# First norm's squares on ScalarE, opening loads in smaller pieces

## The reference

```python
def rmsnorm(x, g):
    x32 = x.astype(F32)
    y = x32 * lax.rsqrt(jnp.mean(x32 * x32, axis=-1, keepdims=True) + EPS)
    return (y * g.astype(F32)).astype(x.dtype)
...
qa, ka, va, qi, ki, wi, cqlat, ckv, kr = split_cols(u @ w_in, AB_SPLITS)   # u = rmsnorm(h, g_mix)
...
k_new = rope(rmsnorm(ka.reshape(nb, t, A_KV_HEADS, A_HEAD_DIM), g_ak), pos)
...
log_a = -RG_C * r * jax.nn.softplus(-lam.astype(F32))                        # layer 1
```

## Time and profile before

| | before |
|---|---|
| median of 3 runs | 2961.33 us (2958.95 to 2961.46) |
| profiled execution, span | 2955.7 us |
| TensorE busy | 2905.3 us, 98% |
| VectorE busy | 1441.9 us, 49% |
| ScalarE busy | 1057.9 us, 36% |
| GpSimd busy | 203.9 us, 7% |
| loads of the weight stream | 742 of 512 KB |
| mean granted clock of TensorE | 0.992 |

### The profile page before, as it was taken

How to read it: one execution, slowest core, us unless ns; L and a number is a source line. 1 busy time by engine, 2 the same in 40 slices (tenths; PEclk the granted TensorE clock), 3 DMA queues, 4 the chain that set the end, 5 groups by cost and what they waited for, 6 DMA issues and landing times.

```text
span 2955.7 us, 45474 instructions
## 1 busy us (share of the span) xinstructions
PE 2905.3 (98%) x18745; PEld 2840.7 (96%) x18745; DVE 1441.9 (49%) x1483; ACT 1057.9 (36%) x1190; POOL 203.9 (7%) x108
## 2 busy tenths in 40 slices
PE   6999899999999999999999999999999999999999
PEld 6999769999999999999999999899999999999999
DVE  7568553643344344334365774446443443443443
ACT  3243432433233233233234642424433432332332
POOL 3100001200000000000120141112000000000000
PEclk9999989999999999999999999999999999999999
DMA  5423004444444444444444444334444444444443
GB/s 190 143 102 122 29 22 134 139 142 141 143 143 143 143 133 145 142 137 142 143 149 145 151 149 143 127 124 151 147 150 151 152 150 141 149 151 147 149 151 132
DMA packets 111355, 405.54 MB, mean 137 GB/s; under 512 B 12497, under 2 KB 13569, under 8 KB 111041
## 3 DMA queue, kind: packets, MB, share of 16 engines
q1 hardware_dynamic: 108000, 392.77, 39.8%
q0 software_dynamic: 1616, 6.35, 0.6%
q10 hardware_dynamic: 1552, 3.60, 0.3%
HBM read 396.58 MB, written 6.09 MB: 136 GB/s over the span
## 4 chain that ended last, share of the span: by engine, by line
PE 96%; DVE 3%; ACT 1%; issue 0%; DMA 0%; SPq 0%; DVEq 0%; ACTq 0%
PE PS L1235 30%; PE PS L1237 30%; PE PS L1236 30%; DVE xl L759 1%; PE PS L1328 1%; DVE w_lo L740 1%; PE PS L1364 1%; PE PS L1525 0%; PE PS L1526 0%; PE PS L1314 0%; PE PS L1502 0%; ACT pr L432 0%; DVE pr L810 0%; PE PS L1311 0%; PE PS L1653 0%
## 5 line engine op out<-in xcount | busy, mean ns | idle before, releaser
L740 DVE TENSOR_TENSOR w_lo<-stage,w_hi 128x1024 fp32r<-128x1024 f32 x742 | 934.2, 1261 | 1245.6 <-ACT w_hi L384 1245.2
L384 ACT ACTIVATE w_hi<-stage 128x1024 fp32r<-128x1024 f32 x742 | 785.6, 1059 | 1700.6 <-PE PS L1237 1692.8
L1235 PE MATMUL PS<-xh,w_hi 128*128 128x336 f32 (+1 forms) x3264 | 1035.3, 317 | 33.1 <-DVE w_lo L740 19.6
L1237 PE MATMUL PS<-xh,w_lo 128*128 128x336 f32 (+1 forms) x3264 | 1028.4, 315 | 0.0
L1236 PE MATMUL PS<-xl,w_hi 128*128 128x336 f32 (+1 forms) x3264 | 1026.5, 314 | 0.0
L1235 PEld LDWEIGHTS PS<-xh,w_hi 128*128 128x128 f32 x3264 | 616.0, 189 | 37.7 <-issue 20.4
L1235 PE MATMUL PS<-hh,w_hi 128*128 128x336 f32 (+1 forms) x2048 | 640.6, 313 | 0.0
L1237 PE MATMUL PS<-hh,w_lo 128*128 128x336 f32 (+1 forms) x2048 | 640.0, 312 | 0.0
L1236 PE MATMUL PS<-hl,w_hi 128*128 128x336 f32 (+1 forms) x2048 | 639.1, 312 | 0.0
L1236 PEld LDWEIGHTS PS<-xl,w_hi 128*128 128x128 f32 x3264 | 619.0, 190 | 1.2
L1237 PEld LDWEIGHTS PS<-xh,w_lo 128*128 128x128 f32 x3264 | 615.8, 189 | 0.0
(11 more groups left out here) (291 smaller groups left out, 1521.0 us busy)
## 6 DMA issues: line engine op xcount, KB each, us to landing
stage<-in_wstream SPq DMA_DIRECT2D x742, 512.0 KB, 3.3
out_y<-x ACTq DMA_DIRECT2D x4, 672.0 KB, 3.5
out_s<-so POOLq DMA_DIRECT2D x8, 256.0 KB, 2.6
x<-in_x_in SPq DMA_DIRECT2D x3, 672.0 KB, 9.7
dmask<-in_ret POOLq DMA_DIRECT2D x4, 360.0 KB, 4.9
s<-in_s_in POOLq DMA_DIRECT2D x1, 1024.0 KB, 5.1
x<-in_x_in SPq DMA_DIRECT2D x2, 336.0 KB, 4.5
tab<-in_tabs SPq DMA_DIRECT2D x1, 672.0 KB, 11.6
```

Of the source, the lines that this page charges most:

```text
L384: act.activation(w_hi[:, s, :], stage[:, s, :], ACT.Copy).then_inc(hi_ready, 1)
L740: dve.tensor_tensor(w_lo[:, s, :], stage[:, s, :], w_hi[:, s, :].bitcast(F32), ALU.subtract).then_inc(lo_ready, 1)
L1235: pe.matmul(out, wh, rh, start=first, stop=False)
L1237: mm = pe.matmul(out, wl, rh, start=False, stop=last)
```

## The change

- Loads: the first half of unit 0 comes first, then tile 0 of x, the second half of unit 0, tile 1, and from there in turn one unit and two tiles of x (nine pieces of x where there were five). ScalarE's queue issues the gains' load, not SyncE's.
- Splits: unit 0 is split in two halves, and the splits of x stand between those of the weights. Tiles 8 and 9 stand behind unit 3, and the last six tiles in the loop of chunk 0, at pieces 4, 5 and 6, on ScalarE and on VectorE.
- TensorE runs nine matmuls of zeros (128 x 512) first, into a bank that nobody reads, and then the first two k-tiles, each with waits of its own.
- Squares: ScalarE squares x four tiles at a time at pieces 4 to 7, into a buffer of its own (`xsq`); GpSimd waits for all four and adds them in a tree of 8, 4, 2 and 1 tiles.
- The sum over partitions comes at the end of chunk 0 (before: after unit 5), as two matmuls of 168 columns; the root at piece 11 (before: 9).
- Softplus: its ScalarE part goes behind the first attention, its VectorE part behind the first quarter of the MLP of layer 0.
- The key steps of chunk 1 move by one piece: 4, 5, 6, 9 to 5, 6, 7, 10, and TensorE's hooks to (1, 2) and (1, 5).

```diff
-        X_PIECES = [(0, 2), (2, 4), (4, 8), (8, 12), (12, 16)]
+        X_PIECES = [(0, 1), (1, 2)] + [(t, t + 2) for t in range(2, KT, 2)]
...
-            sp.dma_start(gains[:], gains_in).then_inc(gains_in_s, 16)
-            for what in ("w0", "x0", "x1", "w1", "x2", "w2", "w3", "x3", "x4"):
-                s = int(what[1])
-                if what[0] == "w":
-                    sp.dma_start(stage[:, s, :], wstream[s]).then_inc(stage_full[s], 16)
-                else:
-                    a, b = X_PIECES[s]
-                    sp.dma_start(x[:, a:b], x_in[:, a:b]).then_inc(x_in_s[s], 16)
+            sp.dma_start(stage[:, 0, 0:512], wstream[0, :, 0:512]).then_inc(w0_first, 16)
+            sp.dma_start(x[:, 0:1], x_in[:, 0:1]).then_inc(x_in_s[0], 16)
+            sp.dma_start(stage[:, 0, 512:UNIT], wstream[0, :, 512:UNIT]).then_inc(stage_full[0], 16)
+            for i in range(1, len(X_PIECES)):
+                a, b = X_PIECES[i]
+                sp.dma_start(x[:, a:b], x_in[:, a:b]).then_inc(x_in_s[i], 16)
+                if i < NR:
+                    sp.dma_start(stage[:, i, :], wstream[i]).then_inc(stage_full[i], 16)
...
+            act.dma_start(gains[:], gains_in).then_inc(gains_in_s, 16)
+
+            def x_piece(i):
+                act.wait_ge(x_in_s[i], 16)
+                norm_tiles(0, *X_PIECES[i])
+
+            act.wait_ge(w0_first, 16)
+            act.activation(w_hi[:, 0, 0:512], stage[:, 0, 0:512], ACT.Copy).then_inc(hi0_first, 1)
             act.wait_ge(gains_in_s, 16)
-
-            lam = gains[:, GAIN["lam"]:GAIN["lam"] + 8]
-            act.activation(spt[:, 0, :], lam, ACT.Abs).then_inc(sp_abs, 1)
-            act.wait_ge(sp_abs, 1)
-            act.activation(spt[:, 1, :], spt[:, 0, :], ACT.Exp, scale=-1.0).then_inc(sp_exp, 1)
-            for u, i_ in ((0, (0, 1)), (1, (2,)), (2, ()), (3, (3, 4))):
+            x_piece(0)
+            act.wait_ge(stage_full[0], 16)
+            act.activation(w_hi[:, 0, 512:UNIT], stage[:, 0, 512:UNIT], ACT.Copy).then_inc(hi_ready, 1)
+            x_piece(1)
+            for u in range(1, NR):
                 split(u)
-                for i in i_:
-                    act.wait_ge(x_in_s[i], 16)
-                    norm_tiles(0, *X_PIECES[i])
+                x_piece(u + 1)
+            x_piece(5)
+
+            def start_piece(j):
+
+                if 4 <= j < 7:
+                    x_piece(j + 2)
+                if 4 <= j < 8:
+                    g = 4 * (j - 4)
+                    act.activation(xsq[:, g:g + 4, :], x[:, g:g + 4, :], ACT.Square).then_inc(xsq_ready, 1)
+
+            def softplus_input():
+
+                lam = gains[:, GAIN["lam"]:GAIN["lam"] + 8]
+                act.activation(spt[:, 0, :], lam, ACT.Abs).then_inc(sp_abs, 1)
+                act.wait_ge(sp_abs, 1)
+                act.activation(spt[:, 1, :], spt[:, 0, :], ACT.Exp, scale=-1.0).then_inc(sp_exp, 1)
...
-                    if g == 0 and j == NR + 5:
-                        rms(0)()
+                    if g == 0:
+                        start_piece(j)
+                    if g == 0 and j == NR + 7:
+                        act.wait_ge(ssum_done, 1)
+                        act.activation(rstd[:].rearrange("p (a b) -> p a b", a=2), PS[:, 0:2, T:T + T // 2], ACT.Sqrt,
+                                       scale=1.0 / D, bias=gcol("eps")).then_inc(rms_ready, 1)
...
+            dve.memset(warm[:].bitcast(F32), 0.0).then_inc(warm_zero, 1)
+            dve.wait_ge(hi0_first, 1)
+            dve.tensor_tensor(w_lo[:, 0, 0:512], stage[:, 0, 0:512], w_hi[:, 0, 0:512].bitcast(F32),
+                              ALU.subtract).then_inc(lo0_first, 1)
             dve.wait_ge(gains_in_s, 16)
-            for u, i_ in ((0, (0, 1)), (1, (2,)), (2, ()), (3, (3, 4))):
+            norm_tiles(0, 0, 1)
+            dve.wait_ge(hi_ready, 1)
+            dve.tensor_tensor(w_lo[:, 0, 512:UNIT], stage[:, 0, 512:UNIT], w_hi[:, 0, 512:UNIT].bitcast(F32),
+                              ALU.subtract).then_inc(lo_ready, 1)
+            norm_tiles(0, 1, 2)
+            for u in range(1, NR):
                 split(u)
-                for i in i_:
-                    norm_tiles(0, *X_PIECES[i])
-
-            u_, z_, z2_ = spt[:, 1, :], spt[:, 2, :], spt[:, 3, :]
-            dve.wait_ge(sp_exp, 1)
-            ch.link(dve.tensor_scalar(z_, u_, 2.0, None, ALU.add))
-            ch.link(dve.reciprocal(z_, z_))
-            ch.link(dve.tensor_tensor(z_, z_, u_, ALU.mult))
-            ch.link(dve.tensor_tensor(z2_, z_, z_, ALU.mult))
-            ch.link(dve.tensor_scalar(u_, z2_, 1.0 / 17, 1.0 / 15, ALU.mult, ALU.add))
-            for k in (13, 11, 9, 7, 5, 3, 1):
-                ch.link(dve.tensor_tensor(u_, u_, z2_, ALU.mult))
-                ch.link(dve.tensor_scalar(u_, u_, 1.0 / k, None, ALU.add))
-            ch.link(dve.tensor_tensor(u_, u_, z_, ALU.mult))
-            lam = gains[:, GAIN["lam"]:GAIN["lam"] + 8]
-            ch.link(dve.tensor_scalar(z_, lam, -1.0, 0.0, ALU.mult, ALU.max))
-            ch.link(dve.scalar_tensor_tensor(u_, u_, 2.0, z_, ALU.mult, ALU.add))
-            dve.tensor_scalar(sp8[:, 0, :], u_, 8.0, None, ALU.mult).then_inc(sp_ready, 1)
-            dve.tensor_scalar(sp8[:, 1, :], u_, -8.0, None, ALU.mult).then_inc(sp_ready, 1)
-
+                norm_tiles(0, 2 * u, 2 * u + 2)
+            norm_tiles(0, 8, 10)
...
+                if g == 0 and 4 <= j < 7:
+                    norm_tiles(0, 2 * j + 2, 2 * j + 4)
...
-                    if j == 6:
+                    if j == 7:
-                    if j == 9:
+                    if j == 10:
...
             mlp(1, U_MLP0, G_MLP0, 0, True)(0)
+            softplus()
...
-                    if (g, k) == (1, 1):
+                    if (g, k) == (1, 2):
...
-                    if (g, k) == (1, 4):
+                    if (g, k) == (1, 5):
...
-                    chunk(U_ABIN, 0, xh, xl, need=need_x(0), hook=sum_squares(0))
-                    pe.wait_ge(rms_ready, 1)
+                    pe.wait_ge(warm_zero, 1)
+                    for n in range(9):
+                        pe.matmul(PS[:, 7, :], warm[:, 0:P], warm[:], start=True, stop=True)
+                    for j in range(2):
+                        if j == 0:
+                            pe.wait_ge(lo0_first, 1)
+                        else:
+                            pe.wait_ge(lo_ready, 1)
+                        pe.wait_ge(xl_ready, j + 1)
+                        mm = product(0, j, j, xh[:, j, :], xl[:, j, :], j == 0, False, 0)
+                    mm.then_inc(unit_done, 1)
+                    chunk(U_ABIN, 0, xh, xl, need=need_x(0), ks=range(1, CU))
+                    pe.wait_ge(const_in, 32)
+                    pe.wait_ge(ssq_ready, 1)
+                    for h in range(2):
+                        mm = pe.matmul(PS[:, h, T:T + T // 2], ones, ssq[:, 0, T // 2 * h:T // 2 * (h + 1)], start=True,
+                                       stop=True)
+                    mm.then_inc(ssum_done, 1)
...
-            sum_squares(0)
+            pool.wait_ge(xsq_ready, 4)
+            for n in (8, 4, 2):
+                ch.link(pool.tensor_tensor(xsq[:, 0:n], xsq[:, 0:n], xsq[:, n:2 * n], ALU.add))
+            pool.tensor_tensor(ssq[:, 0], xsq[:, 0], xsq[:, 1], ALU.add).then_inc(ssq_ready, 1)
```

More of the change, by code:

```diff
@@ L173, in build @@
         A = cur[0]
+        warm = place("warm", [P, 512], A + 30 * TB, F32R)
         xh = place("xh", [P, KT, T], A, F32R)
@@ L191, in build @@
         kn = place("kn", [P, 8, KEYS], B + 12 * TB)
+        xsq = place("xsq", [P, KT, T], B + 12 * TB)
         C = B + 28 * TB
@@ L263, in build @@
         evac = sem("evac")
+        w0_first, hi0_first, lo0_first, warm_zero, xsq_ready = (
+            sem("w0_first"), sem("hi0_first"), sem("lo0_first"), sem("warm_zero"), sem("xsq_ready"))
         const_in = sem("const_in")
-        x_in_s, gains_in_s = [sem(f"x_in_s{i}") for i in range(5)], sem("gains_in_s")
+        x_in_s, gains_in_s = [sem(f"x_in_s{i}") for i in range(9)], sem("gains_in_s")
         x_moved, y_outs = sem("x_moved"), sem("y_outs")
@@ L503, in ab_piece @@
                 if g == 1:
-                    if j == 4:
+                    if j == 5:
                         act.wait_ge(evac, 1)
                         act.activation(sq4[:, 0:3], zt[:, 0:3, :], ACT.Square).then_inc(k_sq, 1)
-                    if j == 6:
+                    if j == 7:
                         act.wait_ge(k_ms, 1)
@@ L578, in _ @@
             attend(0, 0, 0)
+            softplus_input()
             for c in range(2):
@@ new lines, in _, with softplus @@
+            dve.tensor_tensor(w_lo[:, 0, 512:UNIT], stage[:, 0, 512:UNIT], w_hi[:, 0, 512:UNIT].bitcast(F32),
+                              ALU.subtract).then_inc(lo_ready, 1)
+            norm_tiles(0, 1, 2)
+            for u in range(1, NR):
+                split(u)
+                norm_tiles(0, 2 * u, 2 * u + 2)
+            norm_tiles(0, 8, 10)
```

(26 more changed lines are left out.)

5 lines of the change are left out of this document (1 added, 4 removed).

## The result

| | before | after |
|---|---|---|
| median | 2961.39 us (2958.95 to 2965.79) | 2940.78 us (2940.67 to 2941.48) |
| profiled execution, span | 2955.7 us | 2938.7 us |

The ratio is 0.9935, 95% interval 0.9922 to 0.9947: 20.6 us faster, where 10.1 were forecast. Twice as much was gained as the sum says, so either a term of the opening was wrong or the kernel gained where the sum has no term.

What follows compares the result with a forecast made beforehand. TensorE, busy nearly all the span, was taken as the bound, with time to regain only where it stands still. Span 2955.7 - 10.1 = 2945.6, plus 5.6 outside, gave 2951.2 us (chance 0.55), range 2944.5 to 2956.

Steps and rivals of the forecast that it cites:

- Chunk 1's start: Start of chunk 1, after the sum of squares: at 46.2 us instead of 58.84, 12.6 us gained.
- the chain: What ends last in the opening: unit 4 lands at 19.1, last Square ends at 31.0, sum ready at 45.5.
- the tree: GpSimd's four adds of the squares, three VectorE subtractions coming within: 14.5 us; 11.3 without them, 15.3 at most.
- The clock behind the gap: TensorE's slow clock after standing still 8.6 us ahead of chunk 1: 1.7 us lost, bounds 0 and 4.
- The clock behind the key hook: Half clock within 81.4 to 86.4 us, costing 1.6 us: left in as before, though it may go.
- the first rival: Faster still, chance 0.20: subtractions and adds miss each other, clock recovers or slow stretch goes; 14.3 us gained, 2947.0 us.
- The key wait: TensorE's wait ahead of chunk 2 for the key rotation's last step, one unit later: new stall of 0.75 us.
- Norm, softplus, loads: Chunk 0's norm hidden, 1.4 us to spare; moved softplus free, at most 4.5; smaller load pieces allowed 0.2 us.
- the third rival: Opening loads, chance 0.04: four more DMAs cost one after the other, unit 4 lands 7.6 us later; 2958.8 us.
- Sum over all that it named: Chunk 1's start, slow clock and key wait together: 12.6 - 1.7 - 0.75 = 10.1 us faster.
- From there all as before: Everything after the key wait ahead of chunk 2 runs as before, 10 us earlier.
- The base: Time outside the profiled span: median 2961.33 us against span 2955.7, so 5.6 us, carried over unchanged.

Runs made afterwards that it cites:

- poolsq: The kernel after, with the squares and their sum back on GpSimd as before: 2948.12 us, ratio 0.9958.
- softplus: The kernel before, with softplus alone moved as the change moves it: 2961.19 us, ratio 0.9996.
- shift: The kernel before, with only nine matmuls of zeros added ahead of TensorE's first product: 2952.51 us, ratio 0.997.
- pad116: The kernel after, with 116 further matmuls of zeros, 16 columns wide, ahead: 2962.54 us, ratio 1.0012.
- dvesum: The kernel after, with tiles and Squares earlier, key steps at their old pieces, and VectorE adding the squares instead of GpSimd: 2929.75 us, ratio 0.9898.
- pad9: The kernel after, with 9 further matmuls of zeros, 16 columns wide, ahead: 2945.22 us.
- again: The kernel before, unchanged, run and profiled a second time: 2961.28 us, ratio 1.0.
- nowarm: The kernel after, without its nine matmuls of zeros: 2945.64 us.
- tiles: The kernel after, with the last six tiles of x ahead of the split of unit 4 on both engines: 2938.04 us.
- early: The kernel after, with two tiles and two Squares ahead of unit 4, GpSimd adding each group as it comes, key steps at old pieces: 2936.68 us, ratio 0.9921.
- pad64: The kernel after, with 64 further matmuls of zeros, 16 columns wide, ahead: 2945.38 us.

## Why the prediction was wrong

**Chunk 1's start.** Right: 12.06 us earlier, where 12.6 were forecast. Every link of the chain was within 0.6 us. Of the tree, 14.26 us against 14.5: the three subtractions fell into it as assumed (the trace after has three of VectorE's together in the 12.7 us from 32.16). Against the 11.3 us estimated for the tree alone that is 1.0 us for each, a little over the 0.7 to 0.95 of the rows.

**The clock behind the gap.** Right: half clock until 50.4, 1.75 us lost of the 1.7 taken. The 1.7 was my estimate, and no run shows it as such; what the profile of before shows behind its gap is a granted clock of 0.50 until 35.0 us and twelve products in the 3.39 us from 31.77 on, 0.28 us apart, where twelve at 0.155 take 1.86: 1.5 us lost. The row of after, 46.8 to 50.3:

```profile
46.80:50.30 3.50, 3.50 (x14) 3.50 (x13) 2.46 (x2) 0.54 (x1) 0.00 (x0) 0.50 0.26 101
```

**The clock behind the key hook**. Left in as before; it went (the granted clock of 80 to 85 is 1.00), and 1.5 us were gained that the first rival had named. That it went is luck for the sum: nothing in the prediction says when it goes, and in poolsq, with the same hooks, a half clock of 3.4 us stands there.

**The key wait.** 0.6 us, 0.8 with what follows, of the 0.75.

**Norm, softplus, loads.** Hidden, as said. The four more DMAs moved the landing of unit 4 from 19.19 to 19.62 us, not by the 7.6 us of the third rival. That the softplus could leave ScalarE at no price is owed to the table load, which kept its place in idle time and which I had not costed; the experiment softplus shows what it costs otherwise, 1.3 us of ScalarE and a first conversion 1.5 us later.

**Sum over all that it named.** 12.06 - 1.75 + 1.5 - 0.85 = 10.96; 10.66 from 412 to 1012 us. Forecast 10.1; that this is so near owes something to two misses of opposite sign, 0.5 us too much for chunk 1's start and 1.5 too little for the clock.

**From there all as before.** This step failed: the prediction's "from there all as before, 10 us earlier", a term put at nothing without a reason. I took the rest of the kernel, 2860 us, as a constant, and it has four places whose price hangs on where the code lies: 6.4 us between the two profiles, 9.7 between after and the second profile of before (which was also 0.5 us slower in the opening). 5.1 of the 9.7 are the turns themselves; the rest, 4.6, is what three stretches of half clock behind them cost, 3.4 us long each. Where TensorE's code lies changed all of this: the zeros alone shortened the turns (shift), and 116 further matmuls made two long again (pad116). Why a given shift moves the straight fetch by as much as it does is not shown. The trace of before had the rows: the largest waits of TensorE outside the opening, 2.5 to 2.7 us, at the turns. I had cut the view of waits to the first 90 us, and no rival has the mechanism.

**The base.** This failed too. The 5.6 us put outside the span were 2.2, and the other 3.4 were chance, the draw of the profiled execution: a quick execution of a kernel whose runs differ by 10 us. Against a typical one the gain of the opening is 11.2 us and that of the turns 9.7, 20.9 together, and 20.6 is what the medians show.

## What to carry to other kernels

An edit that adds or takes away instructions ahead of a loop can move the fetches of the loop's code; here nine matmuls moved the straight one by 1 to 21 matmuls in front of a turn. So list the engine's waits at each turn in the profile of before, look for two code fetches in the same us, and carry the sum of the turns as a term that can go either way. Compare a span with several executions before anything is put "outside" it. And try a sum that is needed early on the engine whose adds are short, if it has gaps: 6.1 us of adds on VectorE (dvesum) did what 14.3 us on GpSimd could not.

## What the runs showed of the hardware

- A turn of TensorE's loop costs 1.1 to 2.1 us with one fetch of code and 2.6 to 3.2 us with two at once, in all 52 turns of this case's profiles. The next matmul starts 1.61 to 1.77 us after a single packet has landed. A further 1.5 us are lost where half clock follows, which it did behind 11 of the 15 long stops and 1 of the 39 short ones (two of them pad9's second stops). The straight fetch comes every 124 or 125 matmuls, as the median of each profile; 9 matmuls more moved it by 1 to 21 in front of a turn, 64 by 53 to 63, and 116 brought the pair back at two of four turns.
- Nine matmuls that compute nothing made the kernel before 9.9 us faster (shift).
- In pad116 the granted clock fell from 1.00 to 0.50 at 9.4 us, amid matmuls of 16 columns that followed each other without a stop, 0.11 us apart before and 0.21 us behind it; it came back at 29.9 us, amid those of 336 columns.
- The load of ScalarE's table, 1.28 us, ran free in idle time where one wait stood ahead of the first function (it started at 0.76 us in before, at 1.21 in after), and behind the data where two did (at 4.77, softplus).
- shift and pad9 each have some 4 us more in the attention than before and after. Between 310 and 412 us their granted clock is at one half for 27.3 us, that of before, again, after, softplus, nowarm, tiles, early, poolsq, pad64 and pad116 for 20.5 us and that of dvesum for 17.1; at the measured 0.28 us a product against 0.155, 6.8 us more of it lose an estimated 3.0 us, so this is most of the 4 us. First before, then shift:

```profile
310.00:412.00 102.00, 94.16 (x429) 66.30 (x427) 56.27 (x149) 44.35 (x102) 0.00 (x0) 0.90 0.06 21
```

```profile
310.00:412.00 102.00, 94.16 (x408) 66.35 (x407) 53.10 (x136) 41.19 (x90) 0.00 (x0) 0.87 0.07 21
```

- Left open: why two more stretches of half clock fall into the attention of shift and pad9 and not of the others. And pad64's median is 4.6 us behind after's, of which its profile shows 3.3: its turns are those of after to 0.4 us; chunk 1 starts 4.3 us later, since the granted clock was 0.50 from 7.9 to 21.6 us, 1.6 us come back as no half clock follows its shorter gap, and 1.3 are lost again by 412 us.
